# The last projection tiles before four norms, and the first inputs after them, in halves of 256 tokens

## The reference

```python
for i in range(DEPTH_2):                      # 2
    mod = c_act @ w_ada[i] + b_ada[i]
    sh1, sc1, g1, sh2, sc2, g2 = jnp.split(mod, 6, axis=-1)
    h = modulate(rmsnorm(x, norm_mix_g[i]), sh1, sc1)
    m = fourier_mixer(h, w_fourier_out[j]) if i % 2 == 0 else retention_mixer(h, ...)
    x = x + g1[:, None, :] * m
    h = modulate(rmsnorm(x, norm_ffn_g[i]), sh2, sc2)
    x = x + g2[:, None, :] * swiglu(h, w_ffn_in[i], w_ffn_out[i])
shf, scf = jnp.split(c_act @ w_ada_final + b_ada_final, 2, axis=-1)
return modulate(rmsnorm(x, final_norm_g), shf, scf)
```

## Time and profile before

| what | us |
|---|---|
| median of 3 runs | 1632.08 |
| lowest, highest | 1629.43, 1634.11 |
| profiled execution, its own time | 1633.62 |
| its span | 1631.8 |
| TensorE busy | 1576.3 (97%) |
| VectorE busy | 769.6 (47%) |
| ScalarE busy | 599.7 (37%) |
| GpSimd busy | 880.0 (54%) |

### The profile page before, as it was taken

One profiled execution on the slowest core, in us unless ns is written; L12 is line 12 of the kernel. 1 busy time (PEld: TensorE's weight loads), 2 busy tenths in 40 slices (PEclk: granted clock), 3 DMA queues, 4 the chain that ended last, 5 costly groups with the idle time before them and its releaser, 6 DMA issues.

```text
span 1631.8 us, 20940 instructions
## 1 busy us (share of the span) xinstructions
PE 1576.3 (97%) x7110; PEld 1286.6 (79%) x7110; DVE 769.6 (47%) x1048; ACT 599.7 (37%) x857; POOL 880.0 (54%) x1040
## 2 busy tenths in 40 slices
PE   6999999999899999999999999999999999999997
PEld 4678778687688888888878888888876888888885
DVE  6666766786644434443363525424357344111113
ACT  6354433664442222222244434334244322122323
POOL 4555456563756765666553543635534666555551
PEclk9999999999999999999999999999999999999998
DMA  5345335231535555453231321322312454232321
GB/s 194 120 177 193 129 131 201 94 116 41 205 116 193 192 185 189 169 192 116 97 109 65 99 94 53 113 77 88 94 48 67 155 202 143 91 104 90 102 78 52
DMA packets 56935, 202.95 MB, mean 124 GB/s; under 512 B 6320, under 2 KB 6320, under 8 KB 56880
## 3 DMA queue, kind: packets, MB, share of 16 engines
q1 hardware_dynamic: 55728, 198.73, 35.6%
q10 hardware_dynamic: 1152, 3.45, 0.7%
HBM read 200.05 MB, written 2.10 MB: 124 GB/s over the span
## 4 chain that ended last, share of the span: by engine, by line
PE 84%; DVE 7%; issue 3%; ACT 3%; DMA 1%; POOL 1%; DVEq 0%; SPq 0%; ACTq 0%; POOLq 0%
PE banks L1344 23%; PE banks L1348 23%; PE banks L1347 23%; PE banks L1713 2%; PE banks L1717 2%; PE banks L1716 2%; DMA ada_raw<-in_ADA 1%; PE banks L1430 1%; POOL w_lo L352 1%; DVE sqsum L782 1%; PE banks L1753 1%; PE banks L1751 1%; PE banks L1752 1%; DVE X L823 1%; ACT w_hi L376 1%
## 5 line engine op out<-in xcount | busy, mean ns | idle before, releaser
L352 POOL TENSOR_TENSOR w_lo<-w_raw,w_hi 128x256 fp32r<-128x256 f32 x1036 | 879.8, 882 | 721.6 <-ACT w_hi L376 721.5
L376 ACT ACTIVATE w_hi<-w_raw 128x1024 fp32r<-128x1024 f32 x259 | 272.7, 1057 | 680.4 <-PE banks L1344 601.8
L1344 PE MATMUL banks<-a_hi,w_lo 128*128 128x512 f32 x1264 | 500.8, 396 | 0.0
L1348 PE MATMUL banks<-a_hi,w_hi 128*128 128x512 f32 x1264 | 493.2, 390 | 0.0
L1347 PE MATMUL banks<-a_lo,w_hi 128*128 128x512 f32 x1264 | 493.0, 390 | 0.0
L1344 PEld LDWEIGHTS banks<-a_hi,w_lo 128*128 128x128 f32 x1264 | 238.2, 188 | 51.0 <-issue 2.5
L1347 PEld LDWEIGHTS banks<-a_lo,w_hi 128*128 128x128 f32 x1264 | 238.3, 189 | 50.5 <-issue 2.2
L1348 PEld LDWEIGHTS banks<-a_hi,w_hi 128*128 128x128 f32 x1264 | 238.0, 188 | 50.2
L1344 PE MATMUL banks<-b_hi,w_lo 128*128 128x512 f32 x624 | 245.1, 393 | 6.9 <-DVE sq L952 2.7
L1347 PE MATMUL banks<-b_lo,w_hi 128*128 128x512 f32 x624 | 243.4, 390 | 0.0
L1348 PE MATMUL banks<-b_hi,w_hi 128*128 128x512 f32 x624 | 243.3, 390 | 0.0
(11 more groups left out here) (216 smaller groups left out, 1400.6 us busy)
## 6 DMA issues: line engine op xcount, KB each, us to landing
w_raw<-in_W SPq DMA_DIRECT2D x259, 512.0 KB, 3.4
ada_raw<-in_ADA SPq DMA_DIRECT2D x112, 512.0 KB, 4.2
X<-in_XT SPq DMA_DIRECT2D x8, 256.0 KB, 6.1
out<-X SPq DMA_DIRECT2D x8, 256.0 KB, 2.2
scr<-in_DECAY ACTq DMA_DIRECT2D x4, 448.0 KB, 3.3
scr<-in_PT ACTq DMA_DIRECT2D x1, 512.0 KB, 3.5
scr<-in_ROPE ACTq DMA_DIRECT2D x1, 512.0 KB, 4.3
cols<-in_COLS ACTq DMA_DIRECT2D x1, 292.5 KB, 4.4
```

Of the source, the lines that this page charges most:

```text
L352: pool.tensor_tensor(w_lo[:, c % RING, part], w_raw[:, c % RING, part], w_hi[:, c % RING, part].bitcast(fp32), ALU.subtract).then_inc(wlo, 1)
L376: act.activation(w_hi[:, c % RING, :], w_raw[:, c % RING, :], ACT.Copy).then_inc(whi, 1)
L1344: mm = pe.matmul(out, lo, x_hi, start=first, stop=False)
L1348: mm = pe.matmul(out, hi, x_hi, start=False, stop=last)
```

## The change

`KH` = 4 inputs and `HT` = 256 tokens. FRONT is tokens 0 to 255, BACK the rest. `SPLIT` names the tiles made in two halves: tile 7, at ffn1 tiles 6 and 7. Their front halves are made first, into another bank, from all inputs; then the back halves, with the same weights. In the back halves, after `mid` steps (5, at ffn1 7), stands the sum over partitions of the front. `split_start` runs the first four inputs of the next product for the front and then for the back; the sum of the back (`back_stats`) stands after the second tile of the second input of the front. After that `gemm` goes on from the fifth input with 512 tokens. `norm_stats` and the fillers are gone at these norms. `down0b` (v=5) and `down1b` (v=7) get `mid=5` as well.

VectorE and ScalarE do their operations on the halves in the order shown: `split_tile` is the residual, `split_add` the add to `sqsum`, `mult`, `hi` and `lo` are L804, L402 and L795 for one half, `front_rsqrt` and `back_rsqrt` Ln and Exp of a half, `scaled` and `finish` L1319 and L734. ScalarE loads the function table before the front square. It splits the third chunk of the next product (`c + 2`) between the front's high parts, no longer during the projection (`n < 7` becomes `n < 6` at ffn0, `n_hid - 1` becomes `n_hid - 2` at rnorm, `n < 3` becomes `n < 2` at ffn1), and the fourth, as before, ahead of the fifth high part. The output goes out as 16 transfers of 128 KB.

```diff
+HT = S // 2
+KH = 4
+SPLIT = {4: (7,), 5: (7,), 6: (6, 7), 7: (7,)}
+SPLIT_AT = {4: 0, 5: 1, 6: 2, 7: 4}
...
+        front_bank = {4: BANK[TI["fout"] + 1], 5: 6, 6: BANK[TI["retout"] + 1], 7: 6}
+        def front_of(v, m):
+            n = SPLIT[v].index(m)
+            return banks[:, front_bank[v], n * HT:(n + 1) * HT]
...
-            for m in range(KD):
-                sp.wait_ge(x_done, m + 1)
-                sp.dma_start(OUT[:, m, :], X[:, m, :]).then_inc(out_done, 16)
-            sp.wait_ge(out_done, 16 * KD)
+            for h, part in ((half_done, FRONT), (x_done, BACK)):
+                for m in range(KD):
+                    sp.wait_ge(h, m + 1)
+                    sp.dma_start(OUT[:, m, part], X[:, m, part]).then_inc(out_done, 16)
+            sp.wait_ge(out_done, 2 * 16 * KD)
...
+            def split_squares(v, t0):
+                act.preload_act_table_set("natural_log_exp_and_others")
...
+                split_squares(v, t0)
+                front_rsqrt(v)
+                front(0)
+                front(1)
+                back_squares(v, t0)
+                split_w(flat, c + 2)
+                front(2)
+                front(3)
+                back_rsqrt(u)
+                for m in range(KD):
+                    if m == KH:
+                        split_w(flat, c + 3)
+                    act.wait_ge(h_ready, 8 * a + m + 1)
+                    hi(m, BACK if m < KH else slice(0, S))
...
+            split_squares(7, t0)
+            front_rsqrt(7)
...
+            for m in range(2):
+                finish(m, half_scaled, FRONT, half_done)
+            back_squares(7, t0)
+            for m in range(2, 5):
+                finish(m, half_scaled, FRONT, half_done)
+            back_rsqrt(AUX["final"])
+            for m in range(5, KD):
+                finish(m, half_scaled, FRONT, half_done)
             for m in range(KD):
...
+                finish(m, x_scaled, BACK, x_done)
...
+            def front_end(v, t0, g):
+                for m in SPLIT[v]:
+                    split_tile(v, t0, m, g, FRONT, False)
+                for m in SPLIT[v]:
+                    split_add(v, m, FRONT, False)
+            def split_norm(name, v, a, shift, t0, g, gained_by):
...
+                dve.wait_ge(half_r, v - 3)
+                dve.wait_ge(xg_s, 8 * (a + 1) - len(last))
+                mult(0, FRONT)
+                mult(1, FRONT)
+                for m in last:
+                    split_tile(v, t0, m, g, BACK, True)
+                lo(0, FRONT)
+                for m in last:
+                    split_add(v, m, BACK, True)
+                lo(1, FRONT)
+                mult(2, FRONT)
+                mult(3, FRONT)
+                lo(2, FRONT)
+                lo(3, FRONT)
+                for m in last:
+                    wait_read(dve, flat, t0 + m)
+                    gained(name, m, gained_by)
+                dve.wait_ge(r_ready, NORMS[name] + 1)
+                dve.wait_ge(xg_s, 8 * (a + 1))
+                for m in range(KD):
+                    mult(m, BACK if m < KH else slice(0, S))
+                    if m:
+                        lo(m - 1, BACK if m - 1 < KH else slice(0, S))
+                lo(KD - 1, slice(0, S))
...
+            residuals(t0, range(KD - 2), 8, 6, "ffn1", 4, True)
+            add_square(6, KD - 3)
+            front_end(6, t0, 8)
...
+            scaled(0, FRONT, half_scaled)
+            scaled(1, FRONT, half_scaled)
+            split_tile(7, t0, KD - 1, 11, BACK, True)
+            scaled(2, FRONT, half_scaled)
+            split_add(7, KD - 1, BACK, True)
+            for m in range(3, KD):
+                scaled(m, FRONT, half_scaled)
             dve.wait_ge(r_ready, 8)
             for m in range(KD):
+                scaled(m, BACK, x_scaled)
...
+            def part_mul(out, weights, x, part, first, last, signals=None):
+                (_, hi, lo), (x_hi, x_lo) = weights, x
+                mm = pe.matmul(out, lo, x_hi[:, part], start=first, stop=False)
+                if signals is not None:
+                    mm.then_inc(signals, 1)
+                pe.matmul(out, hi, x_lo[:, part], start=False, stop=False)
+                return pe.matmul(out, hi, x_hi[:, part], start=False, stop=last)
+            def split_tiles(v, t0, ks, rhs, ready, mid):
...
+                for m in SPLIT[v]:
+                    out = front_of(v, m)
+                    for n, k in enumerate(ks):
+                        ready(k)
+                        kept[m, k] = chunk_begins(flat, P)
+                        signals = w_used if kept[m, k][0] and not kept_before(kept, m, k) else None
+                        mm = part_mul(out, kept[m, k], rhs(k), FRONT, n == 0, n == len(ks) - 1, signals)
+                mm.then_inc(half_ready, 1)
+                count = 0
+                for m in SPLIT[v]:
+                    out = banks[:, BANK[t0 + m], BACK]
+                    wait_bank(flat, t0 + m)
+                    for n, k in enumerate(ks):
+                        signals = w_used if kept[m, k][0] and kept_before(kept, m, k) else None
+                        mm = part_mul(out, kept[m, k], rhs(k), BACK, n == 0, n == len(ks) - 1, signals)
+                        count += 1
+                        if count == mid:
+                            pe.wait_ge(half_sum, SPLIT_AT[v] + len(SPLIT[v]))
+                            pe.matmul(aux[:, FRONT], ones[:, :], sqsum[:, FRONT], start=True,
+                                      stop=True).then_inc(half_stats, 1)
+                    mm.then_inc(tile_ready, 1)
...
+            def back_stats(v):
+                pe.wait_ge(full_sum, v - 3)
+                pe.wait_ge(half_ln, v - 3)
+                pe.matmul(aux[:, BACK], ones[:, :], sqsum[:, BACK], start=True, stop=True).then_inc(aux_ready, 1)
+            def split_start(t0, a, v, rhs):
+                tiles = {}
+                for part in (FRONT, BACK):
...
+                    for k in range(KH):
+                        x = rhs(k)
+                        x_hi, x_lo = x
+                        for m in range(4):
+                            if part is FRONT:
+                                if k == 0:
+                                    wait_bank(flat, t0 + m)
+                                tiles[k, m] = chunk_begins(flat, P)
+                        if k == 0:
+                            pe.wait_ge(his, base + 1)
+                            for m in range(4):
+                                begins, hi, lo = tiles[k, m]
+                                out = banks[:, BANK[t0 + m], part]
+                                mm = pe.matmul(out, lo, x_hi[:, part], start=part is FRONT, stop=False)
+                                if begins and part is FRONT:
+                                    mm.then_inc(w_used, 1)
+                                pe.matmul(out, hi, x_hi[:, part], start=False, stop=False)
+                            pe.wait_ge(los, base + 1)
+                            for m in range(4):
+                                out = banks[:, BANK[t0 + m], part]
+                                pe.matmul(out, tiles[k, m][1], x_lo[:, part], start=False, stop=False)
+                            continue
+                        pe.wait_ge(los, base + k + 1)
+                        for m in range(4):
+                            signals = w_used if tiles[k, m][0] and part is BACK else None
+                            part_mul(banks[:, BANK[t0 + m], part], tiles[k, m], x, part, False, False, signals)
+                            if part is FRONT and (k, m) == (1, 1):
+                                back_stats(v)
...
+                if split:
+                    split_tiles(split, t0, ks, rhs, ready if ready else lambda k: None, mid)
...
-            gemm(flat, TI["fout"], KD, range(KD), rhs_b, lambda k: pe.wait_ge(f_ready, k + 1))
-            norm_stats(4, "ffn0")
+            gemm(flat, TI["fout"], KD, range(KD), rhs_b, lambda k: pe.wait_ge(f_ready, k + 1), split=4, mid=5)
...
-                 lambda k: pe.wait_ge(y_ready, 4 * (NH - 1) + k + 1))
-            pe.wait_ge(aux_free, AUX["ffn1"])
-            pe.matmul(aux, ones[:, :], cols[:, 0:S], start=True, stop=True)
-            norm_stats(6, "ffn1")
+                 lambda k: pe.wait_ge(y_ready, 4 * (NH - 1) + k + 1), split=6, mid=7)
             swiglu(1, 3, False, 7, "final")
```

163 lines of the change are left out of this document (129 added, 34 removed).

## The result

The changed kernel takes 1622.8 us (median of 11 runs, 1621.0 to 1628.4). The kernel before, timed beside it, takes 1633.6 (11 runs). The ratio is 0.9938, 95% interval 0.9926 to 0.9950: 10.1 us less, between 8.2 and 12.1. Timed a second time (e5) it gave 1624.0 and 0.9939 (0.9921 to 0.9958). The forecast was 1623.8, 8.3 us less. That the two absolute times lie only 1.0 apart is in part luck: the forecast started from 1632.08, the median of three runs, and the eleven give 1633.6. All runs of both kernels taken together (63 before, 17 changed) give 1633.6 and 1623.3, 10.3 us apart, 8.8 to 11.5 by resampling; so the change is worth some 2 us more than forecast. Three executions of 5639, 6678 and 7583 us (the kernel before, e3 and e2) are left out of all medians and ratios. The profiled execution took 1624.42, its span 1622.6 against 1631.8.

The account below looks back on a forecast made before the run. TensorE's matmul stream plus its waits at four norms was taken as the bound. Gains of 3.2 + 0.1 + 4.1 + 0.9 = 8.3 us off the median 1632.08 gave 1623.8 us, range 1620 to 1630.

Parts of the forecast that it names:

- rnorm, 3.2: At rnorm, where VectorE has nothing queued, the fifth input was to start 3.2 us earlier.
- the wait of 0.4 for low part 1: At rnorm, TensorE was to wait 0.4 us for VectorE's low part 1 in the front half.
- ffn0, 0.1: At ffn0, where VectorE is late, the gain was put at 0.1 us, bounds -1 and +1.5.
- ffn1, 4.1: At ffn1, with two split tiles, the back was to end at 1262.7 instead of 1266.84, 4.1 us less.
- the gain from the slow clock: At ffn1, some 1.6 us of the 4.1 were the slow clock's, at 0.50 during sums and first input.
- final, 0.9: At the final norm and output, a gain of 0.9 us, bounds 0 and 1.3.
- The forecast's doubt: At the output, if 1-KB rows went at half the rate, the final norm's gain would be nil.
- Were it not hidden, it would cost 1.28: At rnorm, the table load before the front square is hidden by front matmuls; unhidden it would cost 1.28 us.
- The clock rival: New waits at ffn0 and ffn1 lower TensorE's clock two or three times: gain 3.5 to 5 us, chance 0.2.
- rival 2: Clock falls after the new waits, each costing up to 1.6 us: 1627 to 1628.6 us, chance 0.2.
- The weight-load rival: Half matmuls at 0.19 instead of 0.12 us as weight loads don't overlap: about +19 us, 1651, chance 0.03.
- The small-operations rival: Some 16 half operations per norm path cost 0.2 us more each: 1628 to 1633 us, no change, chance 0.12.

Follow-up runs that it names:

- e5: Changed kernel run again, unaltered; 1624.0 us, ratio 0.9939 to the kernel before.
- e3: Changed kernel with the gains of tiles 4 to 7 moved behind the back half's low parts at all three norms; 1623.9 us, ratio 0.9947.
- e2: Changed kernel with filler matmuls in TensorE's waits at ffn0 and ffn1; 1625.2 us, ratio 0.9954 to the kernel before.
- e8: Kernel before with each output tile sent as two transfers of 1-KB rows; 1635.7 us, ratio 1.0011.
- e9: Kernel before with three fillers delaying the last projection tile ahead of ffn0; 1636.0 us, ratio 1.0019.
- e1: Changed kernel with the split undone at ffn0 alone; 1627.4 us, ratio 0.9963 to the kernel before.
- e4: Changed kernel with ScalarE's split of chunk c+2 moved behind the back half's Exp; 1622.6 us, ratio 0.9944 to the kernel before.
- e10: Changed kernel with three fillers delaying the last projection tile ahead of ffn0; 1624.6 us, ratio 0.9948 to the kernel before.
- e12: Changed kernel with the table load behind the front square at all four norms; 1623.6 us, timed once.
- e7: Changed kernel with the output sent in eight transfers of whole 2-KB rows instead of 16; 1625.1 us, ratio 0.9946 to the kernel before.

## Why the prediction was right, and where it was not

**rnorm, 3.2 against 3.09.** The steps hold: after T0, the front sum at 5.39 (forecast 5.40), Ln 6.02 (6.0), first input 8.09 (8.0), fifth input 20.54 (20.46). Only the wait of 0.4 for low part 1 was under 0.1. What the forecast did not count is that the unsplit kernel can lose more here: in e8 the clock fell at the first input, and the stretch is 25.2, not 23.6. In none of the eleven profiles with the split there did it fall at rnorm. The window of e8 (columns as above):

```profile
828.00:832.00 4.00, 3.97 (x10) 0.57 0.00 0
```

**ffn0, 0.1 against 0.11 and, as the experiments show, up to 3.9.** The mechanism is as put: VectorE late, a wait of 2.58 (2.9 forecast), then a fall of the clock. What failed is a silent premise, that VectorE's lateness of one profile is the kernel's. It depends on when data for the modulation and for the weights arrive, which differs from execution to execution by as much as the effect: 8.9 to 13.6 us between VectorE's first residual and T0. That 0.1 was met to 0.01 is luck, as both profiles of the first pair had VectorE late. The bound of +1.5 was too tight: 3.9 was reached, 1.5 of it by the clock.

**ffn1, 4.1 against 3.44.** The first input came 9.40 after T0 (forecast 9.15), so the front chain holds. The term that failed is the gain from the slow clock. The forecast had it gone from sums and first input; in the changed kernel it fell again after waits of 1.05 and 1.75 and stayed at 0.50 from 1244 to 1250. Where the fall is shorter or absent the stretch is 22.95 to 22.98 (e1, e2, e4, e10, e12), 4.7 less than the first profile of before and 0.5 less than the 23.5 of the forecast, in which the two last gains took 0.9 each; they took 0.48. But the unsplit stretch varies too, 25.8 and 26.0 in e9 and e8, where the clock fell once and not twice. With the long fall on both sides (the first pair) the split is worth 3.4, with the short one on both (e8 and e9 against e1, e4 and e10) 2.8 to 3.1.

**final, 0.9 against 1.08.** The scaling starts 7.05 after T0 (forecast 7.0). ScalarE's finishes take 0.41 each, not 0.45, and end 0.8 earlier than forecast; "about 10 us after the back matmuls" was 8.3 (the forecast's own times give 9). The output gave most of that back: its tail is 3.05 instead of the 2.0 to 2.6 forecast. The smaller backlog came as forecast, 0.46 (from the last issue to the end 1.76 instead of 2.22). But the 16 issues, which the forecast named and put at nothing, cost 0.93: they follow each other each 0.49 us while the finishes come 0.41 apart, so the last is over 1.29 behind the last finish instead of 0.36. The forecast's doubt was about the rows' rate, and that was the wrong term. The Trainium skill (DMA: Bandwidth & Descriptors, "Specifications") puts line rate at 512 B and more; no run here tests that, as the DMA engines were not kept full with 1-KB rows (share 0.80), and the estimate above puts such rows a tenth below the longer ones.

**The table load.** "Were it not hidden, it would cost 1.28" is wrong (e12). The prediction read the load as what released Ln. It ended 0.02 before Ln, but TensorE's sum had ended only 0.12 earlier; taking the load away could give no more than that. The price of GpSimd's company, "up to 1.7 times", is also misread: 1.22 against 0.68 is 1.8.

**The clock rival** came half true: the clock did fall at ffn0 and ffn1, as rival 2 said, and it is the largest scatter in all these kernels. It did not take the gain, since the kernel before falls too (ffn1 in the first profile, all three norms in e8, ffn0 and ffn1 in e9). **The weight-load rival** is out: 0.12 apart. **The small-operations rival** is out at rnorm, where the chain was met to 0.1.

**The sum.** Forecast 8.3, traced 7.7 in one pair, measured 10.1 (8.2 to 12.1) and 9.4 (by the second median). The excess has two places in the profiles, ffn0's split, cheap to underrate from one pair, and the clock at rnorm. By mean stretches of the executions profiled without fillers, delay or another order, whole against split: ffn0 23.7 (before, e1, e8) against 21.9 (changed, e5, e7, e12); rnorm 24.4 (before, e8) against 20.5; ffn1 26.8 (before, e8) against 23.7 (changed, e1, e5, e7, e12); with the final 1.0 that is 9.9. With e9 and e10 counted at rnorm and ffn1 it is 9.4. It is a small sample: one fall of the clock in one profile moves a mean by 0.4 to 0.8, so how the 10.1 divides among the norms is not shown. The first guess for the excess, the early clock fall that the first profile of the changed kernel lacked, is chance: it came back in e5.
